# Biases and first w1 chunk of the next block between the two w2 chunks of a block on TensorE

## The chip, the cores and the metric

The kernel runs on one core of one Trainium2 chip. The metric is device time in microseconds (us) of one execution. The engines are TensorE (PE, with its weight loads as PEld), VectorE (DVE), ScalarE (ACT), GpSimd (POOL) and SyncE (SP), which issues the large transfers from HBM (DMA).

## The reference

One decoder layer on 256 tokens of width 1024, all in float32. It has a token mixer (causal pooling beside a gated DeltaNet), then a mixture of experts: each token goes to 4 of 32 experts, each with a hidden width of 1024 after a clamped SwiGLU.

```python
x = x + gt1 * hybrid_mixer(h, ...)
h = rmsnorm(x, norm_ffn_g[l]) * (1.0 + sc2) + sh2
x = x + gt2 * moe_ffn(h, ...)
...
def expert_block(args):
    tok_b, e = args
    xb = xpad[tok_b]
    hu = xb @ w1[e] + b1[e]
    x_glu = jnp.minimum(hu[:, 0::2], SWIGLU_LIMIT)
    x_lin = jnp.clip(hu[:, 1::2], -SWIGLU_LIMIT, SWIGLU_LIMIT)
    act = x_glu * jax.nn.sigmoid(SWIGLU_ALPHA * x_glu) * (x_lin + 1.0)
    return act @ w2[e] + b2[e]
```

The change is in the mixture of experts alone. w1 of one expert is 1024 x 2048 float32 (8 MB) and w2 is 1024 x 1024 (4 MB).

## The kernel before

The first 388 us compute the mixer, the norm and the router. Then come the experts, block by block. A block is up to 64 tokens of one expert; an expert with more than 64 tokens has two blocks. The block list is data, read from `blocks_i` into registers (`expert_of`, `first_block_of`), and the blocks 1 and up, without the last, run in a hardware loop on each engine (`further_blocks`, L472).

**The ring.** Weights stand in six places ("slots") of 2 MB of SBUF. An expert is six chunks: w1 in slots 0 to 3, w2 in slots 4 and 5. SP issues them in that order, one after the other (`to_ring`, L520). Each first waits for `used[s]`: PE has done its last matmul on what stands in slot s, for all blocks of the expert before. Its landing is told by `landed[s]`. So SP is at most one expert ahead of PE, and a transfer that has to wait holds back all transfers behind it, since SP works in order.

```python
for s in places:
    sp.wait_ge(used[s], blocks_before + USES)
    ...
        sp.dma_start(slot_as(s, 2), chunk_of(e, s)).then_inc(landed[s], 16)
```

**The first experts.** Two further 2 MB places (`spare`) take w2 of experts 1, 2 and 3 early. For them GpSimd copies from spare to slots 4 and 5 (L619 to L628): for each of the two it waits for `used[4]` or `used[5]`, copies, and counts `landed[4]` or `landed[5]` up. Before SP loads w2 of experts 2 and 3 into a spare place it waits for that copy (L550), and only then does it go on to slots 0 to 3 of the same expert:

```python
for e in range(2, EARLY):
    for i in range(2):
        sp.wait_ge(landed[4 + i], 16 * (e + USES))
        to_spare(e, i)
    to_ring(e, range(4), first_block_of(sp, e))
```

**A block on PE.** `bias` (L1373) starts the sums of the hidden layer in banks 0 and 1 with the biases; four `w1_chunk`s (L1392, matmuls at L1384) add to them, and the fourth one's counts release the activation on DVE and ACT; `gather` (L1354) picks the tokens of the next block; `combine` (L1440) adds the block before to the output sums; `turn_sel`, `turn_act`, `turn_x` transpose small tiles, which ACT copies out of PSUM; two `w2_chunk`s (L1428) form the block's output in bank 2. The second of them releases slot 5 and DVE's `y_nat` (L1962), which `combine` of the following block reads. Each chunk is 16 matmul records of 512 columns. The last block has a body of its own (`serve_last`), with the last expert's slots 3 and 5 loaded in two halves each.

**The order on PE** is the order of the code, there is no scheduler.

Of the kernel before, what the change touches and what calls it, by code (L numbers as in the profile page):

```python
# [116 lines left out]
def program(nc, x, c, ada_w, ada_b, norm_mix_g, norm_ffn_g, w_in, conv_w, pool_w, pool_scale, a_log,  # L117
            dt_bias, gdn_norm_g, w_pool_out, w_gdn_out, w_out, router_w, router_b, exp_w1, exp_b1,
            exp_w2, exp_b2, final_norm_g, const, out):
    with ExitStack() as ctx:  # L120
# [5 lines left out]
        def sem(name):  # L126
            return ctx.enter_context(nc.semaphore(name))
# [293 lines left out]
        act_actT = sem("act_actT")  # L421
# [15 lines left out]
        def slot_as(i, c):  # L437
            return ring[:, i, :, :].rearrange("p c n -> p (c n)").rearrange("p (c n) -> p c n", c=c)
# [33 lines left out]
        def further_blocks(eng, body):  # L472

            eng.wait_ge(vec_route, 1)
            last = eng.value_load(blocks_i[0:1, 2 * P + E:2 * P + E + 1], min_val=E - 2, max_val=MAX_BLOCKS - 2) + 1
            with eng.Fori(1, last) as n:
                body(n)
            return last
# [6 lines left out]
        def expert_of(eng, n):  # L485
            return eng.value_load(blocks_i[0:1, bass.ds(n, 1)], min_val=0, max_val=E - 1)
# [362 lines left out]
        def _(pe):  # L849
# [47 lines left out]
            def keep_warm(times, b):  # L897

                for _ in range(times):
                    nc.tensor.matmul(bank[b][:, 0:P], ident, ident, start=True, stop=True)  # L900
# [73 lines left out]
            for i in range(12):  # L974
                n = chunk_no["qkv"][i // 2]
# [46 lines left out]
            for i in range(4):  # L1022
                if i == 3:
                    rates_and_windows()
                n = chunk_no["gate0"][i // 2]
# [15 lines left out]
            n = chunk_no["pool_out"][0]  # L1041
# [235 lines left out]
            for i in range(4):  # L1277
                n = chunk_no["gdn_out"][i // 2]
# [69 lines left out]
            def gather(m):  # L1348

                pe.wait_ge(vec_sel, m + 1)  # L1350
                at_least(pe, act_xT, m)
                for t in range(T):
                    for h in range(2):
                        mm = nc.tensor.matmul(bank[3][h * SLOTS:(h + 1) * SLOTS, :], sel[:, t, :],  # L1354
                                              h2[:, t, h * 512:(h + 1) * 512], start=(t == 0), stop=(t == T - 1))
                mm.then_inc(pe_gather, 1)

            def turn_x(m):
                pe.wait_ge(act_xnat, m + 1)
                for c in range(4):  # L1360
                    mm = nc.tensor.transpose(bank[3][:, c * P:(c + 1) * P], x_nat[:, c * P:(c + 1) * P], ident)  # L1361
                mm.then_inc(pe_xturn, 1)

            def turn_act(n, b):
                pe.wait_ge(vec_act, 2 * n + b + 1)
                for c in range(2):
                    mm = nc.tensor.transpose(bank[b][:, c * P:(c + 1) * P], act_nat[:, b, c * P:(c + 1) * P], ident)
                mm.then_inc(pe_actT, 1)

            def quads(columns, h):  # L1370
                return columns.rearrange("p (f h c) -> p h f c", h=2, c=4)[:, h]

            def bias(n):  # L1373
                pe.wait_ge(act_xT, n + 1)
                pe.wait_ge(vec_onehot, n + 1)
                for h in range(2):
                    for b in range(2):
                        nc.tensor.matmul(bank[b][h * SLOTS:(h + 1) * SLOTS, :], onehot[b * SLOTS:b * SLOTS + E, :],  # L1378
                                         quads(b1_rows[b * SLOTS:b * SLOTS + E, :], h), start=True, stop=False)

            def hidden(n, q, i, b):
                c = 2 * q + i
                for h in range(2):
                    mm = nc.tensor.matmul(bank[b][h * SLOTS:(h + 1) * SLOTS, :], xT[:, c % 4, c // 4, :],  # L1384
                                          quads(slot_as(q, 2)[:, i, b * D:(b + 1) * D], h),
                                          start=False, stop=(c == KC - 1))
                return mm

            def halves_in(e):
                return 16 * ((e + 1) // E + 1)  # L1390

            def w1_chunk(n, q, e=0, last=False):  # L1392
                if q < 3:
                    pe.wait_ge(landed[q], 16 * (e + USES + 1))
                    for i in range(2):
                        for b in range(2):
                            mm = hidden(n, q, i, b)
                    mm.then_inc(used[q], 1)
                    return
                pe.wait_ge(hidden_in, halves_in(e))  # L1400
                if last:
                    for b in range(2):
                        hidden(n, q, 0, b)
                    pe.wait_ge(landed[q], 16 * (e + USES + 1))
                    hidden(n, q, 1, 0).then_inc(pe_hu, 1)
                    hidden(n, q, 1, 1).then_inc(used[q], 1)
                else:
                    pe.wait_ge(landed[q], 16 * (e + USES + 1))
                    for i in range(2):
                        mm = hidden(n, q, i, 0)  # L1410
                    mm.then_inc(pe_hu, 1)
                    for i in range(2):
                        mm = hidden(n, q, i, 1)
                    mm.then_inc(used[q], 1)

            def w2_chunk(n, b, e, last=False):
                pe.wait_ge(act_actT, 2 * n + b + 1)
                if b:
                    pe.wait_ge(last_in, halves_in(e))
                if not last or not b:  # L1420
                    pe.wait_ge(landed[4 + b], 16 * (e + USES + 1))
                for h in range(2):
                    if last and b and h:
                        pe.wait_ge(landed[5], 16 * (e + USES + 1))
                    for c in range(2):
                        for o in range(2):
                            lo = c * D + o * 512
                            mm = nc.tensor.matmul(bank[2][o * SLOTS:(o + 1) * SLOTS, :], actT[:, b, c, h, :],  # L1428
                                                  slot_as(4 + b, 2)[:, h, lo:lo + 512],
                                                  start=(b + h + c == 0), stop=(b + h + c == 3))  # L1430
                mm.then_inc(used[4 + b], 1)

            def combine(n, last=False):

                pe.wait_ge(vec_y, n + 1)
                pe.wait_ge(act_selT, n + 1)
                for t in range(T):
                    for h in range(2):
                        at = slice(h * SLOTS, (h + 1) * SLOTS)
                        mm = nc.tensor.matmul(bank[4 + 2 * t + h][:, :], wselT[at, t * P:(t + 1) * P], y_nat[at, :],  # L1440
                                              start=False, stop=last, skip_group_check=True)
                    if last:
                        mm.then_inc(pe_moe, 1)
# [11 lines left out]
            def turn_sel(n):  # L1455
                pe.wait_ge(vec_wsel, n + 1)
                for t in range(T):
                    mm = nc.tensor.transpose(bank[2][:, t * P:(t + 1) * P],
                                             wsel[:, t].rearrange("p a s -> p (a s)"), ident)
                mm.then_inc(pe_selT, 1)  # L1460

            def finish_block(n, e=0):
                turn_sel(n)
                turn_act(n, 0)
                turn_x(n + 1)
                turn_act(n, 1)
                pe.wait_ge(act_selT, n + 1)
                w2_chunk(n, 0, e)
                w2_chunk(n, 1, e)

            def serve(n):
                e = expert_of(pe, n)
                bias(n)
                for q in range(4):
                    w1_chunk(n, q, e)
                gather(n + 1)
                combine(n - 1)
                finish_block(n, e)

            def serve_last(n):  # L1480
                e = E - 1
                bias(n)
                w1_chunk(n, 0, e)
                w1_chunk(n, 1, e)
                combine(n - 1)
                w1_chunk(n, 2, e)
                turn_sel(n)
                w1_chunk(n, 3, e, last=True)
                keep_warm(5, 3)
                turn_act(n, 0)  # L1490
                keep_warm(2, 3)
                pe.wait_ge(act_selT, n + 1)
                w2_chunk(n, 0, e)
                turn_act(n, 1)
                w2_chunk(n, 1, e, last=True)
# [22 lines left out]
            w1_chunk(0, 3)  # L1518
            gather(1)
            biases_out()  # L1520
            finish_block(0)
            n_last = further_blocks(pe, serve)
            serve_last(n_last)
            combine(n_last, last=True)
# [497 lines left out]
```

## Time and profile before

| | |
|---|---|
| median of 3 runs | 1331.29 us (1330.78 to 1334.29) |
| the profiled execution's own time | 1332.08 us |
| its span, first to last instruction | 1330.3 us |
| PE busy | 1267.3 us (95% of the span) |
| DVE, ACT, POOL busy | 388.4, 181.4, 67.6 us |
| HBM read | 471.97 MB, 356 GB/s over the span |
| granted TensorE clock | 0.997 |

The span is what the trace covers; the execution's own time is 1.8 us more. PE and the transfers are both busy nearly all the time, so the shares alone don't say which sets the pace in which stretch. In the timeline a row merges neighbouring instructions of one line; the start of a row is what counts, since ends of matmuls are modelled.

### The profile page before, as it was taken

What the parts mean: (1) busy time and instruction counts of PE and PEld (TensorE: products, weight loads), DVE (VectorE), ACT (ScalarE), POOL (GpSimd) and SP (SyncE); (2) the same over time, 40 slices, a digit from 0 to 9 for tenths busy, and PEclk for the clock granted to TensorE, in tenths of its full rate; (3) what the DMA queues carried; (4) which work ended last, traced back from release to release, by engine and by line L of the source; (5) the groups of instructions that cost most, each with busy time, mean ns of one, the idle gap of its engine ahead of it and who ended that gap; (6) DMA issues with size and microseconds to landing.
All of it is one profiled execution on the core that took longest, in us unless ns stands there. A gap on an engine that the chain in (4) does not pass through costs nothing.

```text
span 1330.3 us, 17993 instructions
## 1 busy us (share of the span) xinstructions
PE 1267.3 (95%) x6773; PEld 607.9 (46%) x6774; DVE 388.4 (29%) x989; ACT 181.4 (14%) x402; POOL 67.6 (5%) x80
## 2 busy tenths in 40 slices
PE   7999999999999999999999899999999998999997
PEld 5788878788653333333333333333333333333332
DVE  1499655633252221211111121111211111211112
ACT  1110113421121100110000011000110000110001
POOL 1010011110002220000000000000000000000000
PEclk9999999999999999999999999999999999999999
DMA  9998750018389999999999999699999999999995
GB/s 334 338 368 291 265 207 2 17 39 341 120 319 389 428 429 430 428 429 429 427 429 429 428 431 408 271 429 428 430 428 429 429 428 428 430 427 428 430 428 245
DMA packets 62027, 473.52 MB, mean 356 GB/s; under 512 B 4305, under 2 KB 4622, under 8 KB 36906
## 3 DMA queue, kind: packets, MB, share of 16 engines
q1 hardware_dynamic: 60448, 469.48, 85.4%
q10 hardware_dynamic: 1018, 2.48, 0.6%
q0 software_dynamic: 528, 1.10, 0.3%
q8 instruction: 23, 0.38, 0.1%
q14 instruction: 10, 0.08, 0.0%
HBM read 471.97 MB, written 1.07 MB: 356 GB/s over the span
## 4 chain that ended last, share of the span: by engine, by line
PE 59%; DMA 36%; DVE 2%; ACT 1%; SPq 1%; issue 1%; DVEq 0%; ACTq 0%
DMA store<-in_exp_w_dram 34%; PE bank L1384 21%; PE bank L866 13%; PE bank L1428 8%; PE bank L1440 2%; PE bank L1287 2%; PE bank L1354 2%; DMA store<-in_ada_w_dram 2%; PE bank L956 1%; PE bank L1081 1%; PE bank L1378 1%; ACT work L724 1%; PE bank L930 1%; SPq L508 1%; PE bank L1361 1%
## 5 line engine op out<-in xcount | busy, mean ns | idle before, releaser
L1384 PE MATMUL bank<-store,work 128*64 128x512 f32 x2112 | 469.2, 595 | 37.0 <-DMA store<-in_exp_w_dram 36.8
L1384 PEld LDWEIGHTS bank<-store,work 128*64 128x64 f32 x2112 | 148.8, 137 | 352.8 <-issue 319.2
L1428 PE MATMUL bank<-store,work 128*64 128x512 f32 x1056 | 234.1, 595 | 0.9 <-ACT work L809 0.5
L1428 PEld LDWEIGHTS bank<-store,work 128*64 128x64 f32 x1056 | 72.9, 137 | 137.9 <-issue 136.6
L816 ACT ACTIVATE work<-work 128x256 f32<-128x256 f32 x66 | 27.5, 416 | 753.1 <-DVE work L1932 753.1
L866 PE MATMUL bank<-store 128*128 128x256 f32 x576 | 126.9, 380 | 0.0
L1932 DVE TENSOR_SCALAR work<-bank 128x256 f32<-128x256 f32 x66 | 27.6, 419 | 336.3 <-PE bank L1384 336.3
L866 PEld LDWEIGHTS bank<-store 128*128 128x128 f32 x576 | 108.6, 190 | 16.8 <-issue 2.5
L1962 DVE TENSOR_TENSOR work<-bank,work 128x512 f32<-128x512 f32 x33 | 22.8, 692 | 314.0 <-PE bank L1428 314.0
L1440 PE MATMUL bank<-work 64*128 64x512 f32 x264 | 65.6, 615 | 0.8 <-DVE work L1962 0.8
L1354 PE MATMUL bank<-store,work 128*64 128x512 f32 x264 | 62.8, 592 | 0.2 <-DVE work L1870 0.2
L1948 DVE TENSOR_SCALAR work<-consts,region_z 128x128 f32 (+1 forms) x66 | 22.4, 382 | 87.4 <-issue 87.4
L1939 DVE TENSOR_TENSOR work<-work 128x256 f32<-128x256 f32 x66 | 40.7, 617 | 12.3 <-DVE work L1935 12.3
L1440 PEld LDWEIGHTS bank<-work 64*128 64x128 f32 x264 | 22.7, 186 | 43.2 <-issue 41.5
L1354 PEld LDWEIGHTS bank<-store,work 128*64 128x64 f32 x264 | 21.1, 137 | 35.4 <-issue 35.4
L1378 PE MATMUL bank<-work 32*64 32x512 f32 x264 | 35.9, 612 | 0.3 <-issue 0.3
L1561 DVE SCALAR_TENSOR_TENSOR region_z<-store,c_act,region_z 128x512 f32<-128x512 f32 x48 | 35.6, 810 | 0.0
L1594 DVE SCALAR_TENSOR_TENSOR store<-bank,conv_cols,store 128x255 f32<-128x255 f32 (+2 forms) x72 | 31.4, 477 | 1.3
L1081 PE MATMUL bank<-store 128*128 128x256 f32 x128 | 30.4, 386 | 0.0
L956 PE MATMUL bank<-store 128*128 128x256 f32 x128 | 28.8, 382 | 1.3 <-DVE store L1579 1.3
L1935 DVE SCALAR_TENSOR_TENSOR work<-work 128x256 f32<-128x256 f32 x66 | 28.0, 425 | 2.3
L1287 PE MATMUL bank<-store 128*128 128x512 f32 x64 | 28.2, 593 | 0.0
(313 smaller groups left out, 923.6 us busy)
## 6 DMA issues: line engine op xcount, KB each, us to landing
store<-in_exp_w_dram SPq DMA_DIRECT2D x188, 2048.0 KB, 21.9
store<-in_ada_w_dram SPq DMA_DIRECT2D x12, 2048.0 KB, 12.5
store<-in_w_in_dram SPq DMA_DIRECT2D x11, 2048.0 KB, 12.6
store<-in_exp_w_dram SPq DMA_DIRECT2D x8, 1024.0 KB, 14.5
store<-in_w_in_dram SPq DMA_DIRECT2D x4, 1024.0 KB, 17.2
store<-in_w_gdn_out_dram SPq DMA_DIRECT2D x2, 2048.0 KB, 14.2
store<-in_w_out_dram SPq DMA_DIRECT2D x2, 2048.0 KB, 18.3
store<-in_w_pool_out_dram SPq DMA_DIRECT2D x1, 2048.0 KB, 8.1
```

What stands on the lines that cost most here:

```text
L866: mm = nc.tensor.matmul(out_ap, w(k) if w else w_slot(n, j, k), rhs[:, k, :], start=(k == 0), stop=(k == kc - 1))
L956: mm = nc.tensor.matmul(pair(i)[:, a, :], w_slot(n, 2 * (i % 2) + a, k), hT[:, k, :], start=(k + a == 0), stop=(k == KC - 1), skip_group_c ...
L1081: mm = nc.tensor.matmul(pair(7)[:, a, :], w_slot(n, j, k), hT[:, k, :], start=(k == 0), stop=(k == KC - 1))
L1287: mm = nc.tensor.matmul(bank[4 + n][:, :], region_y[:, k, t * P:(t + 1) * P], ring[:, chunk_no["w_out"][h] % RING, k, :], start=(k == 0), ...
L1354: mm = nc.tensor.matmul(bank[3][h * SLOTS:(h + 1) * SLOTS, :], sel[:, t, :], h2[:, t, h * 512:(h + 1) * 512], start=(t == 0), stop=(t == T ...
L1378: nc.tensor.matmul(bank[b][h * SLOTS:(h + 1) * SLOTS, :], onehot[b * SLOTS:b * SLOTS + E, :], quads(b1_rows[b * SLOTS:b * SLOTS + E, :], h ...
L1384: mm = nc.tensor.matmul(bank[b][h * SLOTS:(h + 1) * SLOTS, :], xT[:, c % 4, c // 4, :], quads(slot_as(q, 2)[:, i, b * D:(b + 1) * D], h), ...
L1428: mm = nc.tensor.matmul(bank[2][o * SLOTS:(o + 1) * SLOTS, :], actT[:, b, c, h, :], slot_as(4 + b, 2)[:, h, lo:lo + 512], start=(b + h + c ...
L1440: mm = nc.tensor.matmul(bank[4 + 2 * t + h][:, :], wselT[at, t * P:(t + 1) * P], y_nat[at, :], start=False, stop=last, skip_group_check=True)
L1561: ins = stt(half, w[:, k, :], c_act[:, k:k + 1], half, ALU.mult, ALU.add)
L1594: steps.append(stt(qkv[:, f, shift:S], src[:, a, 0:S - shift], w, qkv[:, f, shift:S], ALU.mult, ALU.add))
L1939: tt(act_nat[:, b, :].rearrange("q (c p) -> q p c", c=2), lin[:, b, :].rearrange("q (p c) -> q p c", c=2), sig[:, b, :].rearrange("q (p c) ...
```

## The change

`serve(n)` begins a block with biases, then w1 chunks 0, 1, 2, 3, and ends with w2 chunks 0 and 1. After the change, the biases and w1 chunk 0 of block n + 1 are issued between w2 chunk 0 and w2 chunk 1 of block n (`begin_block`, called in `finish_block`), and block n + 1 starts at w1 chunk 1. A wait for the second activation tile's copy stands ahead of the biases, since they write the bank it is copied from. PE reads one more block number from `blocks_i` for each block.

```diff
+            def begin_block(n, e):
+                bias(n)
+                w1_chunk(n, 0, e)
+
-            def finish_block(n, e=0):
+            def finish_block(n, e, e_next):
                 turn_sel(n)
                 turn_act(n, 0)
                 turn_x(n + 1)
                 turn_act(n, 1)
                 pe.wait_ge(act_selT, n + 1)
                 w2_chunk(n, 0, e)
+                pe.wait_ge(act_actT, 2 * n + 2)
+                begin_block(n + 1, e_next)
                 w2_chunk(n, 1, e)
 
             def serve(n):
-                e = expert_of(pe, n)
-                bias(n)
-                for q in range(4):
+                e, e_next = expert_of(pe, n), expert_of(pe, n + 1)
+                for q in (1, 2, 3):
                     w1_chunk(n, q, e)
                 gather(n + 1)
                 combine(n - 1)
-                finish_block(n, e)
+                finish_block(n, e, e_next)
 
             def serve_last(n):
                 e = E - 1
-                bias(n)
-                w1_chunk(n, 0, e)
                 w1_chunk(n, 1, e)
                 combine(n - 1)
                 w1_chunk(n, 2, e)
...
-            finish_block(0)
+            finish_block(0, 0, expert_of(pe, 1))
```

On PE, at the end of block 0, ahead of the loop; the waits of an instruction stand behind it (L1428 is w2, L1378 the biases, L1384 w1):

```order
 L1428 MATMUL bank<-store,work 64x512 [waits landed4,act_actT,act_selT]
 L1428 MATMUL bank<-store,work 64x512 x7
+L1378 MATMUL bank<-work 64x512 [waits vec_onehot,act_xT,act_actT]
+L1378 MATMUL bank<-work 64x512 x3
+L1394 ISA
+L1384 MATMUL bank<-store,work 64x512 [waits landed0]
+L1384 MATMUL bank<-store,work 64x512 x7
 L1428 MATMUL bank<-store,work 64x512 [waits landed5,last_in,act_actT]
 L1428 MATMUL bank<-store,work 64x512 x7
```

The eight w2 matmuls that use slot 5, and with them the count that frees it, now stand behind four bias matmuls, eight w1 matmuls and their wait for slot 0.

On PE, from the end of the loop's body (up to L476, its branch) into the last block:

```order
-L1428 MATMUL bank<-store,work 64x512 x16
+L1428 MATMUL bank<-store,work 64x512 x8
+L1378 MATMUL bank<-work 64x512 x4
+L1394 ISA
+L1384 MATMUL bank<-store,work 64x512 x8
+L1428 MATMUL bank<-store,work 64x512 x8
 L476 ISA
 L476 COMPARE_AND_BRANCH
-L1374 REGISTER_ALU
-L1378 MATMUL bank<-work 64x512 x4
-L1384 MATMUL bank<-store,work 64x512 x16
+L1384 MATMUL bank<-store,work 64x512 x8
```

The last block, like every other, now starts with w1 chunk 1; its chunk 0 stands ahead of the w2 chunk 1 of the block before it. No instruction of DVE, ACT, POOL or SP has moved.

## Rows read from the trace of the kernel before

**Rows 1.** The page, 40 slices of the span: DMA engines' busy share in tenths.
```profile
DMA  9998750018389999999999999699999999999995
```

**Rows 2.** Stretches: length, busy us of each engine (instructions), granted clock, DMA share, GB/s.
```profile
591.00:822.00 231.00, 214.67 (x1027) 73.67 (x1022) 39.78 (x110) 23.23 (x55) 0.00 (x0) 1.00 1.01 429
831.70:842.40 10.70, 10.70 (x54) 3.28 (x52) 1.62 (x5) 0.00 (x0) 0.00 (x0) 1.00 0.00 0
986.00:1275.00 289.00, 269.04 (x1288) 92.50 (x1284) 50.03 (x138) 29.14 (x69) 0.00 (x0) 1.00 1.01 428
```

**Rows 3.** The chain that ended last, from 857 us: start, us, what.
```profile
857.37 7.02 PE bank L1428 x32
...
865.40 13.88 PE bank L1384 x64
...
884.16 7.02 PE bank L1428 x32
```

**Rows 4.** PE's register loads (count, ns, first and last start), and ACT's copy.
```profile
L486 PEldq TENSOR_LOAD <-blocks_i x5: 297/300/310, 860.4 to 967.6; - x5
...
884.48 0.38 ACT L809 ACTIVATE work<-bank 128x256 f32<-128x256 f32 x1
```

**Rows 5.** Timeline of PE from 1246 us: start, us, line and tiles, idle before.
```profile
1246.27 3.65 PE L1384 MATMUL bank<-store,work 128*64 128x512 f32 x16 [1.33 <-DMA store<-in_exp_w_dram]
...
1254.73 7.09 PE L1428 MATMUL bank<-store,work 128*64 128x512 f32 x32
...
1275.64 3.65 PE L1384 MATMUL bank<-store,work 128*64 128x512 f32 x16 [1.32 <-DMA store<-in_exp_w_dram]
```

**Rows 6.** SP's issue of slot 0 at 842 us, and its time to landing.
```profile
842.37 0.34 SPq L528 DMA_DIRECT2D store<-in_exp_w_dram  x1
DMA to landing us min/median/max: 7.2/7.2/7.2
```

**Rows 7.** SP's issues of slots 4, 5 and 0; slot 5's to landing.
```profile
861.12 0.33 SPq L528 DMA_DIRECT2D store<-in_exp_w_dram  x1
...
864.56 0.33 SPq L528 DMA_DIRECT2D store<-in_exp_w_dram  x1
DMA to landing us min/median/max: 9.5/9.5/9.5
...
869.16 0.34 SPq L528 DMA_DIRECT2D store<-in_exp_w_dram  x1
```

**Rows 8.** Timeline of PE, POOL and SP from 408 us, SP's with landings.
```profile
408.66 7.09 PE L1428 MATMUL bank<-store,work 128*64 128x512 f32 x32
412.41 0.22 POOL L625 TENSOR_TENSOR store<-store,consts 128x16 f32<-128x16 f32 x1 [45.46 <-PE bank L1428]
416.51 0.21 POOL L625 TENSOR_TENSOR store<-store,consts 128x16 f32<-128x16 f32 x1
416.57 0.33 SPq L531 DMA_DIRECT2D store<-in_exp_w_dram  x1
DMA to landing us min/median/max: 7.7/7.7/7.7
...
421.66 0.33 SPq L528 DMA_DIRECT2D store<-in_exp_w_dram  x1
DMA to landing us min/median/max: 13.4/13.4/13.4
```

**Rows 9.** SP's issue of the last expert's slot 0, and its time to landing.
```profile
1266.46 0.34 SPq L528 DMA_DIRECT2D store<-in_exp_w_dram  x1
DMA to landing us min/median/max: 23.7/23.7/23.7
```

**Rows 10.** Timeline of the last two blocks on PE: start, us, line, idle before.
```profile
1284.10 7.09 PE L1428 MATMUL bank<-store,work 128*64 128x512 f32 x32
...
1292.14 7.09 PE L1384 MATMUL bank<-store,work 128*64 128x512 f32 x32
1299.15 1.99 PE L1440 MATMUL bank<-work 64*128 64x512 f32 x8
```

## The prediction

> **What bounds the kernel now.** I read the busy shares by slice first, then the windows by stretch, then the chain and PE's timeline, then single issues of the weights' queue.
>
> The slices show transfers busy at nine tenths or more from slice 13 on, with one dent in slice 25 [rows 1]. The windows say what that is. From 591 to 822 us and from 986 to 1275 us the DMA share is 1.01 at 428 to 429 GB/s, and PE works 214.67 of 231.00 us and 269.04 of 289.00 us [rows 2]: there the transfers set the pace and PE waits 16.3 and 20.0 us in all. The dent is the one expert with two blocks: from 831.7 to 842.4 us the ring is full and nothing is moved [rows 2]. Behind it PE works without a pause for some blocks, since it is 26.79 us a block (w2 at 857.37, the next at 884.16 [rows 3]) while an expert's transfers take 29.37 us (third-to-fourth-chunk wait ending at 1246.27, the next at 1275.64 [rows 5]), 4.9 us a chunk of 2 MB. So PE catches up 2.6 us a block and then waits again.
>
> The consequence carries the whole forecast: the stream of transfers is the bound. What PE wins or loses inside a block is paid out of its 2.6 us of idleness. Time moves only where **the stream pauses**, and **after the last expert's chunks land**. The change frees slot 0 earlier and slot 5 later, so I go through the places where SP has nothing queued.
>
> **A block in the waiting stretch.** From the chain, 64 w1 records take 13.88 us and 32 w2 records 7.02 until the biases [rows 3]. A chunk of 16 within one kind is thus 13.88 - 7.02 = 6.86, halved 3.43, and going over to another kind of instruction adds 0.16. The biases take 865.40 - 857.37 - 7.02 = 1.01. With w2 at 1254.73 [rows 5], w1 chunk 0 of the next block could start at 1254.73 + 3.43 + 0.16 + 1.01 = 1259.3. Its transfer is three chunks behind the one that ended the wait at 1246.27, so it lands at 1261.0: **a new wait of 1.6 us**. Then come w1 0, w2 1, w1 1 and w1 2, 4 x 3.43, to 1274.7, and the wait at w1 chunk 3 is still there (0.9 us of it), ending at 1275.64 as before. Nothing is gained or lost. Slot 5 is free at 1267.9 instead of 1261.8; its next transfer only starts when slot 4's has landed, near 1280.5. Hidden, with 10 us to spare.
>
> Other edits at no cost: the wait for ACT's copy of tile 1 is over at 884.48 + 0.38 = 884.9, while w2 chunk 0, begun at 884.16, runs to 887.6 [rows 3, 4], cover 2.7 us. The second register load is 0.3 us; PE's sequencer loads at 860.4 what the biases at 864.4 need [rows 3, 4], about 4 us ahead, and without that cover the load would cost 0.3 a block, inside the 0.9. DVE makes `y_nat` 4.6 us later, but `combine` reads it after two to three w1 chunks (7 us or more); behind it on DVE stands `wsel`, wanted later still.
>
> Does putting w1 and w2 in turns cost PE something? A change of kind adds 0.16 us [rows 3], and w1 and w2 have the same tile of 128*64 [rows 5], the biases another. Before and after there are two changes of tile around the biases. If each alternation did cost 0.16, it would be 0.3 a block, again inside 0.9.
>
> **Hole 1, the two-block expert.** Slot 0's count comes one w2 chunk earlier, so the issue at 842.37 [rows 6] moves to 838.9. From a dry queue a chunk takes 7.2 us [rows 6]: it lands at 846.1, not 849.6. But slot 1 still is freed 3.43 after the old time, 845.8, and with the queue dry again it lands at 853.0 (before 854.5). Slots 2 and 3 follow at 857.9 and 862.8. Slot 4 is issued at 861.12 as before [rows 7] and lands at 868.3. So the early start is worth 3.5 us, then 1.4, then 0.8. Then slot 5: before, it was issued at 864.56 and landed 9.5 later, 874.1 [rows 7]. Now biases and w1 chunk 0 go first, 1.01 + 0.16 + 3.43 = 4.6 us, and it is issued at 869.16, where slot 0's was [rows 7]. The queue ran dry at 868.3; it lands at 869.16 + 7.2 = 876.4. **Loss 2.3 us.** The other chunk from an empty queue took 7.7 [rows 8]: bounds 2.3 and 2.8, I take 2.3, the nearer case, the same queue and slot kind. The next expert's slot 5 is issued one block later, 896.0, while slot 4's chunk lands at 876.4 + 5 x 4.9 = 900.9; less the 2.3 us that a dry start costs over a chunk in the stream, the issue is 2.6 us early, and 2.6 more each block. So nothing is lost twice, but nothing is regained either, since the stream then never pauses.
>
> The Trainium skill (DMA: Bandwidth & Descriptors, Anatomy of one DMA) gives a DMA of the GpSimd path a fixed 2.0 us beside bytes over 436 GB/s, most of it behind the last byte. That would be an estimate of 6.8 us for 2 MB and a loss of 1.9 in place of 2.3; the 7.2 of this trace is SP's own, and goes before it.
>
> **Hole 2, behind block 0.** GpSimd copies expert 1's w2 chunk 1 into slot 5 only after `used[5]`, and SP waits for this copy before it fills spare again. Now GpSimd starts it at 416.51, right after the other copy [rows 8]. After the change w2 chunk 1 ends at 408.66 + 3.43 + 0.16 + 1.01 + 6.86 = 420.1; GpSimd follows 0.3 behind (412.41 against the end of w2 chunk 0 at 412.1), and from its start to SP's issue it is 416.57 - 412.41 = 4.16 us. So SP issues at 424.6. The spare transfer before it lands at 416.57 + 7.7 = 424.3: dry queue, landing at 424.6 + 7.2 to 7.7 = 431.8 to 432.3. Before, the chunk behind it landed at 421.66 + 13.4 = 435.1 [rows 8], so this one at 430.2. **Loss 1.6 to 2.1 us, I take 1.9.** Behind the waiting issue stand SP's four w1 chunks of expert 2, which PE needs only from 440 us; but the stream, continuous from here to 831.7, shifts by it, and with it every wait from 591 us on.
>
> **The tail.** The last expert's slot 0 lands at 1266.46 + 23.7 = 1290.2 [rows 9]. Before, PE filled that time with w2 chunk 1 and came to w1 chunk 0 at 1292.14 without a wait; `combine` followed at 1299.15 [rows 10]. Now PE is at w1 chunk 0 at 1284.10 + 3.43 + 0.16 + 1.01 = 1288.7 and stands until 1290.2. Then w1 0, w2 1 and w1 1 are 10.3 + 0.2 us: `combine` at 1300.7. There is no 0.9 to hide it here: PE ran without a pause from the last wait, and the rest (last chunks, activation, w2, output) is a chain behind it. **Loss 1.5 us.**
>
> **Sum**: 2.3 + 1.9 + 1.5 = 5.7 us. The profiled execution took 1332.1, 0.8 above the median, so it would be 1337.8 there, and **1337.0** against the median of 1331.3: +0.43%. A measurement of this kernel tells about 0.3% (4 us) from no change.
>
> **Rivals.**
> - *One hole doesn't open* (13 in 100): a freed slot's transfer overlaps the one before, say because landing is told later than its last bytes. Hole 2 is decided by 0.3 us, though even the overlap then leaves 424.6 against 420.7 issued. Then 1334.8 to 1335.1, within 0.3%.
> - *All hidden* (6): the stream has slack that its share of 1.01 doesn't show, and only the tail is left: 1332.8.
> - *Faster* (4): the chain of transfer and w1 chunk round and round is a loop of latency, and slot 0 freed 3.4 us earlier shortens it. PE's floor is 26.79 a block; over the 16.3 + 20.0 us of waiting [rows 2] the time would fall to 1295. It decides if chunks can land less than 4.9 us apart; 428 GB/s at full share speaks against.
> - *Alternation costs more* (10): if w1 to w2 to w1 adds over 0.45 us a turn, the 0.9 is gone and tail and hole 1 grow by 1 and 0.5: 1338.5 to 1340.
> - *As forecast* (67): 1336 to 1338.5.
>
> The range reaches from one hole missing to costly turns: 1334.0 to 1340.0. Chances: slower 0.78, within 0.3% 0.18, faster 0.04.
>
> **What would show it.** Right: waits for slot 0 of some 1.6 us at every w1 chunk 0 in the stretches at full share; DMA silence that starts anew near 846 and 868 us (plus hole 2's shift); SP's first spare reissue near 424.6; the last expert's `combine` 1.5 us further from the last landing; PE in a block still 26.8. Wrong: landings after 875 us that are not late; PE idle at w1 chunk 3 gone, with PE busier per block; or a stream faster than 429 GB/s.

## The result, and the profile after

The changed kernel takes 1340.58 us (median of 4 runs, 1339.65 to 1342.41) against 1331.12 of the kernel before (median of 4 runs, one more than in the table before): a ratio of 1.0066, with a 95% interval of 1.0054 to 1.0078. It is **slower, by 9 us** (8.8 by the ratio, 9.5 by the medians). The forecast had slower, and 5.7 us: the sign and the three places are right, the size is short, and 1340.58 lies just above the upper end of the stated range, 1340.0. The profiled execution took 1339.87 us with a span of 1338.0, 7.8 us over the profile before.

The page of the changed kernel, in 40 slices: clock granted to PE, and the DMA engines' share. The dent of [rows 1] is now two slices wide.

```profile
PEclk8999999999999999999999999999999999999999
DMA  9998650018288999999999998799999999999995
```

The stretches of [rows 2] again: the transfers run at the same rate, and PE is idle for the same 16 and 20 us (231.00 - 214.97 and 289.00 - 269.12). The new thing is the granted clock, 0.99 in both; the last row is one piece of the first stretch, at half the clock.

```profile
591.00:822.00 231.00, 214.97 (x1020) 74.87 (x1018) 39.95 (x108) 23.65 (x56) 0.00 (x0) 0.99 1.01 429
986.00:1275.00 289.00, 269.12 (x1282) 93.67 (x1280) 50.16 (x136) 29.57 (x70) 0.00 (x0) 0.99 1.01 428
663.90:667.30 3.40, 3.40 (x10) 0.98 (x8) 0.00 (x0) 0.00 (x0) 0.00 (x0) 0.50 1.00 424
```

A block in the waiting stretch, timeline of PE (answers to [rows 5]). Between the biases and w1 chunk 0 stands the new wait, and the second w2 chunk follows behind it:

```profile
1231.61 3.65 PE L1428 MATMUL bank<-store,work 128*64 128x512 f32 x16
1235.20 1.09 PE L1378 MATMUL bank<-work 32*64 32x512 f32 x8
1237.74 3.65 PE L1384 MATMUL bank<-store,work 128*64 128x512 f32 x16 [1.46 <-DMA store<-in_exp_w_dram]
1241.23 3.60 PE L1428 MATMUL bank<-store,work 128*64 128x512 f32 x16
1244.66 5.75 PE L1384 MATMUL bank<-store,work 128*64 128x512 f32 x26
```

Behind block 0, timeline of GpSimd and SP, with the second spare transfer's time to landing (answers to [rows 8]):

```profile
416.19 0.33 SPq L531 DMA_DIRECT2D store<-in_exp_w_dram  x1
420.52 0.22 POOL L625 TENSOR_TENSOR store<-store,consts 128x16 f32<-128x16 f32 x1 [4.35 <-PE bank L1428]
424.68 0.33 SPq L531 DMA_DIRECT2D store<-in_exp_w_dram  x1
DMA to landing us min/median/max: 7.8/7.8/7.8
```

GpSimd, which before went from one copy to the next, now stands 4.35 us for w2 chunk 1. From SP's first spare issue to the landing of its second it is 424.68 - 416.19 + 7.84 = 16.3 us; before it was 13.6.

Behind the two-block expert, SP's issue of slot 5 (answers to [rows 7]), and PE's w1 chunk 0 of block 15, the first of the two blocks of that expert, at whose end the pause begins:

```profile
872.67 0.33 SPq L528 DMA_DIRECT2D store<-in_exp_w_dram  x1
DMA to landing us min/median/max: 7.7/7.7/7.7
...
810.12 5.35 PE L1384 MATMUL bank<-store,work 128*64 128x512 f32 x16 [1.47 <-DMA store<-in_exp_w_dram]
```

Slot 5 met an empty queue (slot 4's chunk landed at 872.72, just behind the issue): 7.7 us to landing where it was 9.5. And 16 w1 matmuls took 5.35 us instead of 3.65.

The tail, timeline of PE (answers to [rows 10]):

```profile
1296.49 3.65 PE L1384 MATMUL bank<-store,work 128*64 128x512 f32 x16 [1.46 <-DMA store<-in_exp_w_dram]
...
1306.95 1.99 PE L1440 MATMUL bank<-work 64*128 64x512 f32 x8
```

I cut the last part of each profile into three pieces; a landing is issue time plus time to landing. **A** is from SP's first spare issue behind block 0 to the landing of the last chunk before the pause of the two-block expert (slot 5 of expert 15). **B** is from there to the landing of the last chunk of all, **C** from there to the end of the span. What lies before the first cut (the mixer) differs by up to 6 us between the profiles; the change touches nothing there. The ratio is that of the timed runs, each kernel against the kernel before timed beside it, whose median was 1331.1 to 1333.2 us. One execution of the kernel with slot 0 ahead of the second spare took 3371.5 us, against 1335.3 to 1341.4 in its five others, and is left out of its numbers.

| kernel | A | B | C | ratio to before, interval |
|---|---|---|---|---|
| before | 415.1 | 483.1 | 15.5 | 1 |
| changed | 418.3 | 486.5 | 17.0 | 1.0066 (1.0054 to 1.0078) |
| changed, once more | 418.6 | 486.6 | 17.0 | 1.0065 (1.0052 to 1.0078) |
| block 0 old | 416.3 | 485.8 | 17.0 | 1.0040 (1.0027 to 1.0053) |
| block 16 old | 418.8 | 483.8 | 17.0 | 1.0045 (1.0033 to 1.0057) |
| block 31 old | 418.3 | 486.9 | 15.1 | 1.0054 (1.0038 to 1.0070) |
| blocks 0, 16, 31 old | 416.7 | 484.7 | 15.5 | 1.0009 (1.0000 to 1.0019) |
| control, all old, written out | 416.5 | 484.3 | 15.5 | 1.0016 (1.0005 to 1.0027) |
| slot 0 ahead of second spare | 415.4 | 485.7 | 18.7 | 1.0036 (1.0023 to 1.0049) |
| wait filled with matmuls | 420.4 | 488.6 | 17.0 | 1.0086 (1.0071 to 1.0100) |
| late spare, old order | 415.6 | 477.7 | 15.7 | 0.9960 (0.9947 to 0.9973) |
| late spare, new order | 418.4 | 481.0 | 18.9 | 1.0008 (0.9998 to 1.0018) |

The changed kernel's loss in the profile is 3.2 + 3.4 + 1.5 = 8.1 us, less 0.4 us that it had gained by chance before the first cut. Taken once more, where 7 to 10 us over the kernel before and the same pauses were expected, it is 9 us over with the same parts (3.5, 3.5 and 1.5).

### The profile page after: what moved, and what is told of

Read it like the earlier page. It is cut to its first block, busy times and chain, and to the rows that moved or that the text cites. A ratio compares the mean times of both kernels' runs of the same rounds, so it can differ in the third digit from the quotient of the medians.

```text
span 1338.0 us, 18121 instructions
## 1 busy us (share of the span) xinstructions
PE 1272.1 (95%) x6773; PEld 611.8 (46%) x6774; DVE 387.4 (29%) x989; ACT 181.4 (14%) x402; POOL 67.7 (5%) x80
## 4 chain that ended last, share of the span: by engine, by line
PE 59%; DMA 34%; SPq 3%; DVE 2%; issue 1%; ACT 1%; DVEq 0%; ACTq 0%
DMA store<-in_exp_w_dram 32%; PE bank L1384 19%; PE bank L866 13%; PE bank L1428 11%; PE bank L1287 2%; DMA store<-in_ada_w_dram 2%; PE bank L1440 2%; PE bank L1354 2%; PE bank L956 1%; PE bank L1081 1%; PE bank L1378 1%; SPq L528 1%; SPq L489 1%; ACT work L724 1%; SPq L508 1%
## 5 line engine op out<-in xcount | busy, mean ns | idle before, releaser
L1384 PE MATMUL bank<-store,work 128*64 128x512 f32 x2112 | 477.4, 602 | 40.9 <-DMA store<-in_exp_w_dram 40.9
L1384 PEld LDWEIGHTS bank<-store,work 128*64 128x64 f32 x2112 | 151.9, 138 | 357.9 <-issue 306.6
L1428 PE MATMUL bank<-store,work 128*64 128x512 f32 x1056 | 239.6, 596 | 0.9 <-ACT work L809 0.5
L1428 PEld LDWEIGHTS bank<-store,work 128*64 128x64 f32 x1056 | 73.0, 137 | 137.9 <-issue 136.6
L1354 PE MATMUL bank<-store,work 128*64 128x512 f32 x264 | 62.8, 593 | 0.2 <-DVE work L1873 0.2
L1354 PEld LDWEIGHTS bank<-store,work 128*64 128x64 f32 x264 | 20.9, 137 | 35.5 <-issue 35.5
L1378 PE MATMUL bank<-work 32*64 32x512 f32 x264 | 35.9, 613 | 0.3 <-issue 0.3
```

## The experiments

### One place at a time back in the old order

`finish_block` got a switch, and the blocks of interest were written out between pieces of the loop:

```diff
-            def finish_block(n, e, e_next):
+            def finish_block(n, e, e_next, between=True):
...
+                if between:
+                    pe.wait_ge(act_actT, 2 * n + 2)
+                    begin_block(n + 1, e_next)
+                    w2_chunk(n, 1, e)
+                else:
+                    w2_chunk(n, 1, e)
+                    begin_block(n + 1, e_next)
```

**Block 0 old** (`finish_block(0, ..., between=False)`).

> The changed kernel, but block 0 ends in the old order (both w2 chunks, then biases and w1 chunk 0 of block 1). Theory of the holes: SP's reissue to spare goes back to about 420.7 us, the stream's shift before the two-block expert (2.85 us in the changed kernel) falls to about 0, and the time is some 2.5 to 2.9 us under the changed kernel's, with the pause behind block 16 and the tail unchanged. Rival (the alternation of w1 and w2 or the clock costs PE time in every block, and the place of block 0 is no matter): within 0.7 us of the changed kernel, and the stream as late as there.

SP's second spare issue of this kernel:

```profile
424.70 0.33 SPq L531 DMA_DIRECT2D store<-in_exp_w_dram  x1
DMA to landing us min/median/max: 9.3/9.3/9.3
```

The first issue stood at 420.61 here, so the second comes 4.09 us behind it, as before, and lands 13.4 behind it, not 16.3. The time fell by 0.0026 of the ratio, 3.5 us, more than expected but with intervals of 0.0013 on either side. A fell by 2.0 to 2.4 only: one chunk of expert 2 landed 6.2 us behind the one ahead of it, beside a fetch of instructions (below), where it was 5.5 and 5.7 in the two profiles of the changed kernel. The first theory holds, the rival (no matter which block) falls.

**Block 16 old**, the second block of the two-block expert.

> The changed kernel, but block 16 alone, the second block of the two-block expert, ends in the old order. Theory of the holes: slot 5 of the next expert is issued 4.6 us earlier, its landing is not late against the landings ahead of it beyond 0.5 us, and the time is 2.3 to 3.4 us under the changed kernel's. Rival (slot 5 is not what is late, but PE as a whole, by the low clock at 810 us): 0 to 0.7 us under the changed kernel's.

```profile
867.02 0.33 SPq L528 DMA_DIRECT2D store<-in_exp_w_dram  x1
DMA to landing us min/median/max: 9.4/9.4/9.4
```

Slot 5 is queued in time again (9.4 us, as the 9.5 of [rows 7]). It lands 42.3 us behind the last chunk before the pause, where it was 42.4 before and 45.9 in the changed kernel. B fell by 2.8 us, the ratio by 0.0021, 2.8 us; the two intervals of the ratio just overlap, so the landings carry this reading. Not all of it is slot 5's queue: no low clock fell near 810 us in this profile, which is worth 0.7 us (see the clock), and two chunks beside fetches of instructions cost some back. Still the rival (PE is late as a whole, 0 to 0.7 us) falls.

**Block 31 old.**

> The changed kernel, but block 31 alone, the last but one, ends in the old order. Theory of the tail: combine of the last block goes back to where it stands before the change, counted from the last landings, and the time is 1.5 us under the changed kernel's (span from the last landing to the end 15.5 instead of 16.95 us). Rival (the tail is set by the last chunk's landing): the same distance from last landing to end as in the changed kernel, 0 us gained.

In the timeline of PE, w1 chunks 0 and 1 and `combine` of the last block:

```profile
1296.84 3.65 PE L1384 MATMUL bank<-store,work 128*64 128x512 f32 x16
1300.69 3.65 PE L1384 MATMUL bank<-store,work 128*64 128x512 f32 x16 [0.20 <-DMA store<-in_exp_w_dram]
1304.28 1.99 PE L1440 MATMUL bank<-work 64*128 64x512 f32 x8
```

The wait ahead of chunk 0 is gone, and `combine` is 7.4 us behind its start, near the 7.0 of [rows 10] (in the changed kernel w2 chunk 1 lies between them too, 10.5 us). C fell by 1.9 us to 15.1 (here the last chunks landed a little later against PE, so it is even 0.4 under before), the ratio by 0.0011 to 0.0012, 1.5 us. As expected; here too the parts show it, since the intervals of the ratios overlap.

**All three old.**

> The changed kernel, but blocks 0, 16 and 31 end in the old order, the other 29 in the new one. Theory of three places: the whole loss is there, so the time is that of the kernel before within 1 us (with block 15's earlier slot 0 worth up to 0.8 us the other way). Rival (each block in the new order costs something, by the alternation on PE or by drops of the granted clock at the longer wait): over 2 us slower than before, with as many low-clock intervals as the changed kernel (4 between 600 and 1200 us).

The ratio is 1.0009: 0.0057 of the 0.0066 is gone with three of 32 placements. But 1.0009 is 1.2 us (the medians say 1.5), a little outside the 1 us expected and short of the rival's 2, and A is still 1.6 and B 1.6 us over before. That called for a control: the same code written out, but **every** block old.

> A control for the kernel with blocks 0, 16 and 31 in the old order: the same code written out outside the loop, but every block in the old order. If the written-out copies cost something (three more 16 KB fetches of instructions on the transfers' engines, which lie beside late chunks at 865, 891 us), this kernel is 1 to 3 us slower than before, and that kernel's residue is the writing out. If they cost nothing, it is within 0.5 us of before and the other 29 blocks in the new order cost the residue. No low-clock intervals between 600 and 1200 us if these belong to the new order's longer wait.

The control is slower than before by 0.0016, 2.1 us, and has A 1.4 and B 1.2 us longer. So the residue of the kernel with three old blocks is there without a single block in the new order, and the other 29 blocks cost nothing that can be measured: the two intervals overlap. Of the residue, B's part has a further fetch of instructions beside a late chunk (last section). A's has none: it is one chunk of expert 2 that landed 6.4 us behind the one ahead of it, beside a fetch near 440 us that the kernel before has too, where it was 5.1. The expectation was right on this, and right that the clock stays up: the control has no low-clock interval between 600 and 1200 us, while the one with three old blocks has three there.

### The queue behind block 0

For experts 2 and 3, SP takes slot 0, which the new order frees early, between the two spare transfers:

```diff
+                before = first_block_of(sp, e)
                 for i in range(2):
                     sp.wait_ge(landed[4 + i], 16 * (e + USES))
                     to_spare(e, i)
-                to_ring(e, range(4), first_block_of(sp, e))
+                    if not i:
+                        to_ring(e, range(1), before)
+                to_ring(e, range(1, 4), before)
```

> The changed kernel, but for experts 2 and 3 SP issues w1 chunk 0 between the two transfers to spare, so that something is queued while GpSimd's copy is late. Theory (the late copy starves the queue behind block 0): the pause there goes, the chunks of expert 2 land 2.4 us or more earlier, and the time is 2.4 to 3.3 us under the changed kernel's. Rival (the stream is slow there for another reason, such as GpSimd's copying or the fetch of instructions): the same total gap, 0 us gained.

SP's second spare issue of this kernel:

```profile
428.23 0.33 SPq L531 DMA_DIRECT2D store<-in_exp_w_dram  x1
DMA to landing us min/median/max: 9.1/9.1/9.1
```

GpSimd's copy is as late as ever (the issue is 8.5 us behind the first one, at 419.75), but now the queue isn't empty: 9.1 us to landing, of which it waited in the queue for part. A is 415.4, within 0.3 of before. The ratio falls by 0.0029, 3.9 us, and the median from 1340.9 to 1337.6, 3.3 us, at the upper end of what was expected or a little over. So the loss behind block 0 is the empty queue, not the copying.

### The clock

The profile after has four intervals of 3.4 us between 600 and 1200 us in which PE was granted 0.5, the lower of its two levels (1.2 in place of 2.4 GHz): from 663.9, 810.7, 1032.6 and 1179.3 us. Before there was none between 16 and 1327 us. Each stands on a w1 chunk 0, and starts within 1 us of the end of its 1.5 us wait; so do all 39 such intervals of the eight profiles that have this wait. To see whether the wait makes them, five matmuls of the identity were put into it:

```diff
             def begin_block(n, e):
                 bias(n)
+                keep_warm(5, 3)
                 w1_chunk(n, 0, e)
```

> The changed kernel with five 128-column matmuls of the identity (some 1.4 us) between the biases and w1 chunk 0, in the wait for slot 0; they compute nothing that is used. Theory (the granted clock falls after the new 1.5 us wait): no or at most one low-clock interval between 600 and 1200 us instead of 4, the wait for slot 0 down to 0.3 us or less. The matmuls delay slot 5 in the pauses by 1.4 us more each, so the time is 1 to 3 us over the changed kernel's. Rival (the clock falls for a reason outside PE's waits): as many low-clock intervals as without.

The stretch from 600 to 1340 us of this kernel, and PE's waits from 600 to 840 us (total, times, longest):

```profile
600.00:1340.00 740.00, 726.07 (x3594) 271.45 (x3590) 132.84 (x360) 77.94 (x185) 0.00 (x0) 1.00 0.97 411
...
PE bank L1384 <- DMA store<-in_exp_w_dram: 4.1, 9, 0.8
```

In the changed kernel such waits were 16.0 us, 14 of them, from 591 to 822 us, the longest 1.5. With the wait filled no interval of low clock is left between 60 and 1340 us. So they come with the wait for slot 0 standing idle; filling it costs more than they do (2.8 us more than the changed kernel by the medians of 1343.7 and 1340.9, as expected), since the matmuls delay slots 4 and 5 further where the queue runs dry. What in this wait does it is not separated. PE waits 1.46 us there and 0.82 at w1 chunk 3, where before it waited 0.79 and 1.33 in a block: the longest wait has grown by 0.13 us only. What stands ahead of it has changed too, 1.0 us of biases on 32 rows where it was w1 matmuls on 128.

What a low interval costs depends on where it falls. A chunk takes 5.35 instead of 3.65 us, 1.7 more. In the waiting stretch the 0.8 us left at w1 chunk 3 takes half of it and the next wait most of the rest (behind the interval at 663.9 us that wait was 0.82 and not 1.46). At 810.7 us it fell on the block before the pause, and PE's counts came 0.7 us late into the pause: slot 5 was issued at 872.67, 38.2 us behind the last landing ahead of the pause (issued at 819.08, 15.4 to landing), where the forecast has 869.16 - 831.7 = 37.5. The other profiles bear this out: the changed kernel taken once more, with a low interval at 812.2 us, has 38.1, and three with block 16 in the new order and none near (block 0 old, block 31 old, slot 0 ahead of the second spare) have 37.5 each. In the kernel with slot 0 ahead of the second spare one began at 1296.5 us, on the last block: C is 18.7 there and not 17.0, and that execution took 1341.4 us against a median of 1337.6.

### Filling the pause itself

The experiments say that pauses of the stream are what this kernel pays for, and the largest was there before the change: 13 us at the two-block expert. The two spare places lie idle from expert 4 on. In this version, with the **old** order on PE, SP and GpSimd use them again for experts 16 to 20:

```diff
+LATE = range(16, 21)
...
-            with sp.Fori(EARLY, E - 1) as e:
+            with sp.Fori(EARLY, LATE[0]) as e:
                 to_ring(e, range(6), first_block_of(sp, e))
+            for e in LATE:
+                for i in range(2):
+                    sp.wait_ge(landed[4 + i], 16 * ((EARLY if e == LATE[0] else e) + USES))
+                    to_spare(e, i)
+                to_ring(e, range(4), first_block_of(sp, e))
+            with sp.Fori(LATE[-1] + 1, E - 1) as e:
+                to_ring(e, range(6), first_block_of(sp, e))
...
-            for e in range(1, EARLY):
+            for k, e in enumerate([*range(1, EARLY), *LATE]):
...
-                    pool.wait_ge(upper_in[i], 16 * (e + 1))
+                    pool.wait_ge(upper_in[i], 16 * (k + 2))
```

> The kernel before with its order on PE, and the two spare places used once more: for experts 16 to 20 SP loads w2 to spare, and GpSimd copies it to slots 4 and 5, as it does for experts 1 to 3. If the pauses of the stream are what costs time, the 13 us pause at the two-block expert is partly filled: spare takes two chunks there, slot 0 of expert 16 still lands at 849.6, a pause of some 3 us remains on each side, and the time is 5 to 6.5 us under the kernel before. Rival (PE is what bounds from there on, or GpSimd's copies slow PE or the transfers): within 1 us of the kernel before.

Two stretches of its trace; where the DMA share was 0.00 for 10.7 us [rows 2], two short dips are left:

```profile
843.00:851.00 8.00, 8.00 (x40) 2.69 (x38) 0.36 (x3) 0.00 (x0) 0.00 (x0) 1.00 0.83 328
866.00:875.00 9.00, 9.00 (x48) 2.88 (x42) 2.32 (x5) 0.00 (x0) 4.64 (x6) 1.00 0.83 308
```

B fell by 5.4 us, and the time to 1327.2 us, a ratio of 0.9960 (0.9947 to 0.9973): **faster than both kernels**, in the range expected (5.2 us by the medians). PE is not the bound behind the pause, and GpSimd's 40 us of further copies cost nothing that shows.

The same with the changed kernel's order:

> The changed kernel with the same use of spare for experts 16 to 20. If the changed order's loss at the two-block expert is one of slot 5 freed late to a dry queue, it remains to be paid by GpSimd's copy of expert 17's w2, which waits for the same slot 5: the loss against the kernel with late spare and the old order stays 7 to 9 us. Rival (the further lookahead hides it): 3 us less, 4.5 to 6 us.

It takes 1333.0 us, 5.8 us (by the ratios 0.0048, 6.4) over the one with the old order. By the medians that is in the rival's range, 4.5 to 6, by the ratios between it and the first one's 7 to 9. The parts speak for the first: A is 2.8 and B 3.3 us longer, as without late spare. But its profile has a low clock on the last block (C 18.9) and took 1338.2 us, the longest of its twelve runs. I leave this one open.

## Why the prediction was right, and where it was short

The mechanism and the three places held. Short were the sizes of two of the sum's three terms, 1.9 and 2.3 us where A and B are 3.2 and 3.4 longer, and the clock was not in it.

- **The stream is the bound, and time moves only at its pauses and behind its end**: shown, by the 29 of 32 placements that cost nothing measurable and by the landings, at which each of the three others gave its part back.
- **A block in the waiting stretch**: a new wait of 1.6 us was forecast with 0.9 left at w1 chunk 3, 1.46 and 0.82 measured, and nothing lost there. What I had not seen is the clock after it.
- **Behind block 0**: forecast 1.9 us (1.6 to 2.1), measured 2.8 at the second spare landing and 3.2 at the end of A. Mis-sized in two parts. GpSimd started 0.5 us later than worked out (4.33 against 3.83 behind SP's first issue; PE was on time, but GpSimd followed the end of w2 chunk 1 by 0.7 us and not by 0.3, and why is open), and the spare chunk took 7.8 to landing, past my upper bound of 7.7. The remaining 0.4 is mostly a chunk that landed 5.5 us behind the one ahead of it (5.1 before), beside the fetch near 440 us; since it was 6.4 in the control, in the old order, nothing ties it to the change.
- **The two-block expert**: forecast 2.3 us (2.3 to 2.8), measured 3.4 over B. The 7.2 us from an empty queue was the wrong one of my two values. I called it the nearer case, for its queue and kind of slot; but it was a chunk of w1, and slot 5 gets w2, as the spare place does that took 7.7. Slot 5 took 7.7. In all twelve profiles the chunks issued to a queue that was empty, or at most 0.4 us from it, took 7.1 to 7.3 us if they were of w1 (20 chunks) and 7.5 to 8.0 if of w2 (16). Why, no run shows. That makes 2.8, and where block 0 was old and no low clock fell near, slot 5 landed 45.2 us behind the last chunk before the pause, 2.8 over before's 42.4. The other 0.7 is the low clock at 810.7 us. Slot 4's chunk landed 0.9 us later than worked out, so the queue ran dry only as slot 5 was issued and not before; that changes nothing in the sum.
- **The tail**: forecast 1.5 us, measured 1.5.
- **Not in the sum at all**: the clock. I took PE's idle time as free because its total stays the same; but waits of 1.5 and 0.8 us stand where waits of 0.8 and 1.3 were, and behind the first of them the clock fell in some blocks. The term was put at nothing; 0.7 us at the two-block expert is what it cost in the profile, and a profile with one in the tail lost 1.7 more. How often a run has one there is not measured. The medians are 9 us apart and the profiles 7.8, but that difference is within what the part before the first cut varies by, and shows nothing.
- **Rivals**: one hole not opening, all hidden, and faster are each ruled out by the timed ratio and by the landings. Costly alternation, whose 1338.5 to 1340 came nearest to the measured time, is ruled out too: in the block above, w1 chunk 0 takes 3.49 us until w2 chunk 1 starts and that one 3.43 until w1 chunk 1 (1237.74, 1241.23, 1244.66), so a turn costs 0.06 at most, not 0.45. And `combine` of the last block stood 10.46 us behind w1 chunk 0, with three chunks between, against 10.3 + 0.2 worked out.

## What to carry to other kernels

When a stream of transfers is the bound, an order on an engine is judged by when it frees each buffer of the ring, at the few places where the queue can run dry; list those places first and price each with the time from an empty queue, measured on the same kind of chunk; where there is none, carry the larger value. Freeing one buffer early and another late isn't neutral: the queue is served in order, so the late one decides. Idle time of an engine that is off the bound is not free if a change moves it and makes one wait longer: look whether TensorE's clock holds. And a pause that was there before the change can be worth more than the change: here filling it gave 5 us.

## What the runs showed of the hardware

- A 2 MB transfer whose queue was empty or nearly so took 7.1 to 7.3 us from issue to landing if it was a chunk of w1, and 7.5 to 8.0 if of w2. In a full stream a chunk of either landed 4.9 us behind the one ahead of it.
- Waits of 0.8 and 1.3 us in a block left TensorE's clock up for 1300 us; with waits of 1.5 us behind the biases and 0.8 in their place it fell to the lower level for 3.4 us, each time right behind the 1.5 us, but only 3 to 7 times in a profile with 12 to 16 such waits; often 147 us, that is five blocks, apart.
- Code written out beyond the loop costs a kernel that lives on its transfers. The control, all blocks in the old order, is 2 us slower. Its trace has three fetches of instructions that the kernel before lacks, near 863, 889 and 1290 us, on the transfers' engines. Beside the first a chunk landed 6.3 us behind the last one, beside the other two 4.9 as ever. From 860 to 870 us:

```profile
q1 hardware_dynamic: 287, 4.19, 98.4%
q8 instruction: 1, 0.02, 0.6%
```

A packet of 0.02 MB is no load by itself; that it is what delays the chunk is argued from where it stands, not shown, and how 2 us come of it isn't shown either.
